# Decay masks of a Mamba-2 scan moved into the spare rows of its one-hot products, with a new order of work in two mixers of a four-block model

## The chip, the cores and the metric

One core of a Trainium2 chip runs the whole program in one launch. The metric is the time of the launch on the device in microseconds (us), less is better. TensorE is called PE below, VectorE DVE, ScalarE ACT, GpSimd POOL and SyncE SP.

## What is computed

256 tokens of width 1024 pass through two stacks of two layers. A layer of the first stack is a gated feed-forward, a mixer and another feed-forward; a layer of the second stack is one hybrid layer, which the change does not touch. The mixer adds three branches: a two-direction Mamba-2 scan (16 heads of 64, 2 groups, state 128, chunks of 128), latent attention of 8 heads, and a gated depthwise convolution. The reference of the scan, cut to what matters:

```python
x = x + 0.5 * swiglu(rms_norm(x, ffn1_norm[l]), ...)
u = rms_norm(x, mix_norm[l]) @ w_in[l]
z, xbc, dt_raw, q_lat, kv_lat, k_pe, c_h, c_b, c_c = jnp.split(u, pts, axis=-1)
...
# ssd_chunked, one direction; the second runs on flipped inputs
a_cs = jnp.cumsum(dtc * a, axis=2)
seg = a_cs[:, :, :, None] - a_cs[:, :, None, :]
decay = jnp.exp(jnp.where(lower, seg, -jnp.inf))
cb = jnp.einsum('bclgn,bcsgn->bclsg', cc, bc)
y_diag = jnp.einsum('bclsg,bclsgr,bcsgrp->bclgrp', cb, decay, xc * dtc[..., None])
decay_states = jnp.exp(a_cs[:, :, -1:] - a_cs)
states = jnp.einsum('bclgn,bclgr,bclgrp->bcgrpn', bc, decay_states, xd)
chunk_decay = jnp.exp(a_cs[:, :, -1])
...
y_off = jnp.einsum('bclgn,bcgrpn,bclgr->bclgrp', cc, prev, jnp.exp(a_cs))
```

## The kernel before

**Weights.** Every weight matrix comes in blocks of 512 KB. SP loads them into a ring of eight slots (RAW), ACT rounds a block (WH), DVE subtracts to get the rest (WL), both some five blocks ahead of PE, and PE multiplies three times (high by high, low by high, high by low). A block is 24 products of 256 columns or 12 of 512 and keeps PE busy for about 2.8 us. Its operands read XTH, XTL, WH and WL in the profile, FR in the mixer's output product. Other products are in plain fp32 or on rounded data.

**Order.** The class `Order` writes the order of all phases for all engines before the program is built. Chains of phases (`rows`, `decay`, `qk`, `mla_head`, `states`, `segment`, `finish` and so on in `mix`) are laid between the weight blocks. `WORK` gives each phase a duration per engine, `LEAD` each chain a lead, `RULE` the due times. An engine then works through its list strictly in order and waits on semaphores. In a mixer the phases that need a bank of PSUM take turns on banks 0 and 1, later 0, 1 and 3 (from `heads`), then 2 and 3 (after `mo_a` of the second half); weight blocks use banks 4 to 7.

**The attention** of a mixer runs head by head: `sc` (QTK,QTQ) makes scores, DVE finds their maximum (STATS), ACT takes exponentials (MP), `pt` transposes them (CONSTS,MP), ACT copies (MPT), `pv` multiplies by MV. `mo_a` divides (MO), and four flips transpose MO at the end.

**The scan.** `decay` makes dt (DT) and dt times a (DA). `cum` sums DA along the tokens by four products with triangles; ACT and DVE split the result into LBH. `ex` makes, by eight products of 16 columns, the sums that become the factors EX, and DVE makes the bias BI = ln dt - sum. `xs`, `btk` and `cbm` transpose the convolved input XC and form CB. `state` (XDD,BTK) and `fin` (STT,XC) carry the state across the chunks; DVE evicts `fin` to YT. `seg(n)`, n = 0 to 15, makes for two heads and both directions the decay matrix of 128 x 128: a product adds the mask (ROUNDED, 512 columns), two products spread the rows of LBH (256 columns each), then ACT takes four exponentials of 128 columns with the bias BI (ET), DVE adds the two directions and multiplies by CB. `apply(n)` multiplies by XS. The convolution branch has `cn_a` (CHC, RS, SPREAD), for which ACT takes a square root and DVE a reciprocal (RS).

In the profile L1190 is the helper of all products, L1187 that of all transposes, L1602 that of all activations, and L2068 the DVE split; the tiles tell them apart.

Of the kernel before, what the change touches and what calls it, by code (L numbers as in the profile page):

```python
# [58 lines left out]
def constants():  # L59
# [185 lines left out]
class Order:  # L245
# [307 lines left out]
    def mix(self, i, l):  # L553
# [315 lines left out]
class Kernel:  # L869
# [61 lines left out]
    def allocate(self):  # L931
# [216 lines left out]
class PE:  # L1148
# [229 lines left out]
    def cum(self, i):  # L1378
        k, w = self.k, self.w
        b, ps = self.tbank(("cum", i), "cum_dve", i)  # L1380
        w.wait_ge(*self.at("const6", 0))
# [1 line left out]
        for t in range(2):
            for d in range(2):
                m = self.mm(ps[:, 256 * t + 128 * d:256 * t + 128 * d + 128], k.DA[:, t, d, :], (k.LE, k.GE)[d],
                            t == 0 and d == 0, True)
        m.then_inc(*self.up("cum_pe", i))

    def ex(self, i):
        k = self.k  # L1390
        b, ps = self.tbank(("ex", i), "ex_dve", i)
        for t in range(2):
            for d in range(2):
                at = 64 * t + 32 * d
# [184 lines left out]
class Scalar:  # L1579
# [261 lines left out]
    def cum(self, i):  # L1841
# [1136 lines left out]
```

## Time and profile before

| | us |
|---|---|
| median of 3 runs (lowest, highest) | 1837.5 (1834.53, 1838.35) |
| the profiled execution | 1835.07 |
| its span | 1833.3 |
| PE busy | 1813.2 |
| DVE busy | 1263.2 |
| ACT busy | 1080.0 |
| POOL busy | 105.8 |

The granted clock of TensorE is 1.00 of full speed over the whole span. The mean DMA rate is 169 GB/s. The first mixer lies at about 192 to 404 us of the span, the second begins at about 769 us. In a row of the timeline the number after the start is the length of a group of instructions; matmuls overlap, so what a group costs is best read from its start to the start of the next group. A number in brackets is idle time of the engine before the group, and what ended it. fp32 products are two records each, so that "x8" of CONSTS,DA is four products.

### The profile page before, as it was taken

To read this page: it belongs to the slowest core of one execution; us is meant where nothing else is said; L and a number is where in the kernel's file an instruction comes from. 1 tells how busy PE (TensorE), PEld (TensorE's weight loads), DVE (VectorE), ACT (ScalarE), POOL (GpSimd) and SP (SyncE) were. 2 spreads that over 40 slices of the span, in tenths; PEclk is the share of its full clock that TensorE was granted. 3 is DMA by queue.
4 is the path that set the end of the run, shared out by engine and by line. 5 is a ranking of instruction groups with operands and counts; after the bars stand their busy time and mean duration, and the time that the engine had idled before them with its cause. 6 is when DMAs were issued, how large, how long until landed. Compare 5 with 4: busy or idle time off the path is not lost.

```text
span 1833.3 us, 28507 instructions
## 1 busy us (share of the span) xinstructions
PE 1813.2 (99%) x11518; PEld 1613.1 (88%) x11518; DVE 1263.2 (69%) x1932; ACT 1080.0 (59%) x1675; POOL 105.8 (6%) x83
## 2 busy tenths in 40 slices
PE   9999999999999999999999999999999999999999
PEld 9998998789998999899789998988778888887887
DVE  6765797876665665587876665687767567875755
ACT  6444667764444444575776444576776456668742
POOL 0000110010000000020000000002101000210100
PEclk9999999999999999999999999999999999999999
DMA  7565543245555555553335555554445555544463
GB/s 275 194 194 188 188 151 106 93 152 193 193 193 186 188 196 195 191 185 103 103 109 191 179 195 194 169 188 140 160 136 172 189 166 181 170 138 138 161 195 127
DMA packets 86596, 310.08 MB, mean 169 GB/s; under 512 B 9648, under 2 KB 10288, under 8 KB 86464
## 3 DMA queue, kind: packets, MB, share of 16 engines
q1 hardware_dynamic: 85680, 306.35, 50.5%
q8 instruction: 91, 1.49, 0.3%
q0 software_dynamic: 496, 1.65, 0.2%
q14 instruction: 41, 0.34, 0.1%
q10 hardware_dynamic: 288, 0.25, 0.0%
HBM read 307.16 MB, written 1.05 MB: 168 GB/s over the span
## 4 chain that ended last, share of the span: by engine, by line
PE 90%; ACT 5%; DVE 3%; issue 1%; DMA 0%; POOL 0%; SPq 0%; DVEq 0%; ACTq 0%
PE bank L1190 87%; PE bank L1187 3%; ACT PA L1602 2%; ACT WH L1602 1%; DVE WL L2068 1%; ACT L1602 1%; ACT ET L1602 1%; DVE PA L2721 0%; ACT MP L1602 0%; ACT FR L1602 0%; DMA X<-in_x_dram 0%; DVE PC L2746 0%; DVE STATS L2414 0%; ACT BZ L1602 0%; ACT ZS L1602 0%
## 5 line engine op out<-in xcount | busy, mean ns | idle before, releaser
L2068 DVE TENSOR_TENSOR WL<-RAW,WH 128x1024 fp32r<-128x1024 f32 x585 | 703.9, 1213 | 400.1 <-ACT WH L1602 398.5
L1602 ACT ACTIVATE WH<-RAW 128x1024 fp32r<-128x1024 f32 (+2 forms) x587 | 608.6, 1049 | 475.0 <-PE bank L1190 473.1
L1190 PE MATMUL bank<-WH,FR 128*128 128x512 f32 x1264 | 318.3, 390 | 1.4 <-ACT FR L1602 1.4
L1190 PEld LDWEIGHTS bank<-WH,FR 128*128 128x128 f32 x1264 | 233.8, 188 | 48.4 <-issue 1.8
L1190 PE MATMUL bank<-XTH,WH 128*128 128x256 f32 x1792 | 254.1, 279 | 0.6 <-ACT XTH L1602 0.6
L1190 PE MATMUL bank<-XTH,WL 128*128 128x256 f32 x1792 | 251.0, 277 | 0.0
L1190 PE MATMUL bank<-XTL,WH 128*128 128x256 f32 x1792 | 250.9, 277 | 0.0
L1190 PEld LDWEIGHTS bank<-XTH,WH 128*128 128x128 f32 x1792 | 226.9, 188 | 1.7 <-issue 0.8
L1190 PEld LDWEIGHTS bank<-XTL,WH 128*128 128x128 f32 x1792 | 225.8, 188 | 0.0
L1190 PEld LDWEIGHTS bank<-XTH,WL 128*128 128x128 f32 x1792 | 225.8, 188 | 0.0
L1190 PE MATMUL bank<-WL,FR 128*128 128x512 f32 x632 | 173.1, 388 | 0.0
L1190 PE MATMUL bank<-WH,XTHS 128*128 128x512 f32 x576 | 165.3, 398 | 2.5 <-ACT WH L1602 2.5
L1190 PE MATMUL bank<-WL,XTHS 128*128 128x512 f32 x576 | 160.3, 390 | 0.1
L1190 PE MATMUL bank<-WH,XTLS 128*128 128x512 f32 x576 | 160.2, 390 | 0.0
L1190 PEld LDWEIGHTS bank<-WL,FR 128*128 128x128 f32 x632 | 118.4, 188 | 24.6
L1190 PEld LDWEIGHTS bank<-WL,XTHS 128*128 128x128 f32 x576 | 108.0, 188 | 23.7 <-DVE WL L2068 1.0
L1190 PEld LDWEIGHTS bank<-WH,XTLS 128*128 128x128 f32 x576 | 108.1, 188 | 23.1
L1190 PEld LDWEIGHTS bank<-WH,XTHS 128*128 128x128 f32 x576 | 104.0, 188 | 24.6 <-ACT WH L1602 3.4
L2822 POOL TENSOR_TENSOR STATS<-STATS,HALFS 128x1 f32<-128x1 f32 (+2 forms) x36 | 68.8, 1921 | 683.5 <-DVE STATS L2763 191.0
L1602 ACT ACT_TABLE_LOAD x49 | 62.9, 1283 | 2.5 <-PEq L2969 1.7
L2253 DVE SCALAR_TENSOR_TENSOR XC<-XBG,COLP,XC 128x256 f32<-128x256 f32 x96 | 46.5, 484 | 8.6 <-ACT XC L1602 5.6
L1602 ACT ACTIVATE PA<-PA,STATS 128x128 f32<-128x128 f32 x64 | 34.2, 536 | 24.0 <-DVE STATS L2727 24.0
(328 smaller groups left out, 1827.3 us busy)
## 6 DMA issues: line engine op xcount, KB each, us to landing
RAW<-in_WALL_dram SPq DMA_DIRECT2D x569, 512.0 KB, 3.3
RAW<-in_WALL_dram SPq DMA_DIRECT2D x8, 448.0 KB, 3.3
RAW<-in_WALL_dram SPq DMA_DIRECT2D x8, 256.0 KB, 2.9
X<-in_x_dram SPq DMA_DIRECT2D x4, 256.0 KB, 5.4
out_dram<-X SPq DMA_DIRECT2D x4, 256.0 KB, 2.0
ROWP<-in_ROWP_dram POOLq DMA_DIRECT2D x1, 672.0 KB, 11.5
CONSTS<-in_CST_dram POOLq DMA_DIRECT2D x1, 664.0 KB, 7.8
ROUNDED<-in_CSTR_dram POOLq DMA_DIRECT2D x1, 208.0 KB, 12.7
```

Of the source, the lines that this page charges most:

```text
L1187: return self.e.transpose(out, in_, self.k.EYE[0:rows, 0:rows])
L1190: return self.e.matmul(out, lhs, rhs, start=start, stop=stop, skip_group_check=True)
L1602: return self.e.activation(out, in_, func, **k)
L2068: self.e.tensor_tensor(lo, raw, hi.bitcast(F32), ALU.subtract).then_inc(*self.up("lo", j))
L2253: e.scalar_tensor_tensor(o, src[:, tap:tap + 256], k.col("ssd_conv_w", l, 12 * tap + ch), o, ALU.mult, ALU.add).then_inc(*self.up("conv_dv ...
L2822: self.e.tensor_tensor(st, st, k.HM[:, 0:n], ALU.pow).then_inc(*self.up("rsqrt_pool", key))
```

## The change

`seg` no longer has a mask product and a bias. The one-hot stationary tiles are replaced by TOX and FROMX, 16 x 128 columns each, whose 64 spare rows hold "runs"; the other operands LBT and LBF hold the split sums in their used rows and the cut values in their spare rows. Four products of 256 columns give the whole exponent, and ACT takes one exponential of 512 columns. `cum` now adds ln dt inside the product (eight fp32 products instead of four) and is evicted in two halves by ACT and DVE. `ex` does both tiles in one product (four products of 32 columns instead of eight of 16), and its DVE step is gone. `decay` writes ln dt and dt times a into more places. POOL loads TOX, FROMX and the constant rows of LBF and LBT (2.4 MB in four DMAs) in each mixer, after the last two `sc`, in the phase `scan_load`; every `seg` waits for them. The leads of all chains of the mixer and its rule are new numbers; `heads` waits for `cum` instead of `ex`, and `ex` comes ahead of `cum`.

```diff
@@ def scan_constants
+    ends = [(1, 2)] + [(2 * j, 2 * j + 2) for j in range(1, 63)] + [(126, 127)]
+    runs = np.stack([(i >= a) & (i <= b) for a, b in ends]).astype(np.float32)
...
+        for p in (64 * x, 64 * x + 32):
+            s[x, p + i[:16], i[:16]] = 1
+        s[x, 64 * (1 - x):64 * (1 - x) + 64] = runs[:, None, :]
...
@@ WORK
-    "cum": "P90 A60 V70", "ex": "P170 A27 V20", ... "seg": "P56 A104 V90"
+    "cum": "P198 A105 V140", "ex": "P90 A27", ... "seg": "P50 A61 V90"
@@ LEAD["mix"], RULE
-        "qk": 1670, "mla_head": 180, "rope1": -470, "decay": 150, "states": 210, "segment": 70, "finish": 10, ...
+        "qk": -860, "mla_head": 230, "rope1": 1250, "decay": -10, "states": 220, "segment": -130, "finish": -110, ...
-RULE = {"ffn": (60, 240, 40), "mix": (400, 0, 60), "hyb": (500, 0, 20)}
+RULE = {"ffn": (60, 240, 40), "mix": (360, 0, 60), "hyb": (500, 0, 20)}
@@ Order.mix
+            yield [("ex", i)]
             yield [("cum", i)]
-            yield [("ex", i)]
...
-            yield "ex", i
+            yield "cum", i
...
-            yield [("mo_a", i, 1), ("tbanks", (2, 3))]
+            yield [("mo_a", i, 1), ("scan_load", i), ("tbanks", (2, 3))]
@@ PE.cum
+        w.wait_ge(*self.at("decay_act", (i, "ln")))
+                self.mm(o, k.DA[:, t, d, :], (k.LE, k.GE)[d], t == 0 and d == 0, False)
+                m = self.mm(o, k.LN[:, t, d, :], k.EYE, False, True)
@@ PE.ex
-                self.mm(ps[:, at:at + 16], (k.LE, k.GE)[d], k.DA[:, t, d, 0:16], t == 0 and d == 0, True)
-                m = self.mm(ps[:, at + 16:at + 32], (k.GT, k.LT)[d], k.DA[:, t, d, 0:16], False, True)
+                m = self.mm(out[:, :, d, a, :], tri, k.DA[:, :, d, 0:16], d == 0 and a == 0, True)
@@ PE.seg
-        w.wait_ge(*self.at("const5", 0))
-        self.mm(ps, k.EYER, k.CUT.unsqueeze(2).to_broadcast([128, 2, 2, 128]), True, False)
+        w.wait_ge(*self.at("scan_in", i))
         for x in range(2):
-            m = self.mm(ps[:, :, x, :], k.TO[:, h0 + x:h0 + x + 1].to_broadcast([128, 128]),
-                        k.LBH[:, 256 * t:256 * t + 256].rearrange("p (d s) -> p d s", d=2), False, x == 1)
+            self.mm(ps[:, :, x, :], k.TOX[:, h0 + x, :], k.LBT[:, 256 * t:256 * t + 256].rearrange("p (d s) -> p d s", d=2),
+                    x == 0, False)
+        for d in range(2):
+            m = self.mm(ps[:, d, :, :], k.LBF[:, 256 * t + 128 * d:256 * t + 128 * d + 128], k.FROMX[:, h0:h0 + 2, :], False, d == 1)
@@ Scalar.cum, Scalar.seg
-        self.act(k.LBH[:, :], ps[:, :], ACT.Copy).then_inc(*self.up("cum_act", i))
+        self.act(k.LBT[0:64, :], ps[0:64, :], ACT.Copy)
+        self.act(k.LBF[64:128, :], ps[64:128, :], ACT.Copy).then_inc(*self.up("cum_act", i))
...
-                m = self.act(k.ET[:, n % 4, at:at + 128], k.PS[k.bank["seg", i, n]][:, at:at + 128], ACT.Exp,
-                             bias=k.BI[:, t, d, h:h + 1])
+        self.act(k.ET[:, n % 4, :], k.PS[k.bank["seg", i, n]][:, :], ACT.Exp).then_inc(*self.up("et_act", (i, n)))
@@ Vector.ex (gone)
-        e.tensor_tensor(k.BI, k.BI, ps, ALU.subtract).then_inc(*self.up("ex_dve", i))
@@ Pool.scan_load
+        for h in (6, 7):
+            w.wait_ge(*self.at("sc_pe", (i, h)))
+        w.wait_ge(*self.at("cum_pe", i))
+        w.wait_ge(*self.at("kpe_pool", (i, 1)))
+        e.dma_start(k.TOX[:, :, :], src[:, 0:2048].rearrange("p (h s) -> p h s", h=16)).then_inc(*k.sig.landed("scan_in"))
+        e.dma_start(k.FROMX[:, :, :], src[:, 2048:4096].rearrange("p (h s) -> p h s", h=16)).then_inc(*k.sig.landed("scan_in"))
+        e.dma_start(k.LBF[0:64, :], src[0:64, 4096:4608]).then_inc(*k.sig.landed("scan_in"))
+        e.dma_start(k.LBT[64:128, :], src[64:128, 4096:4608]).then_inc(*k.sig.landed("scan_in", i))
```

What the new numbers do to the order of work is seen in the instruction lists. The first place is PE at the end of the attention of a mixer. QTK,QTQ is `sc`, CONSTS,MP `pt`, MV,MPT `pv`, CONSTS,XC `xs` (and `btk`), XC by XC `cbm`, and WH or WL by XTH a weight block. Before:

```order
L1187 MATMUL bank<-CONSTS,XC 128x128 x8
L1190 MATMUL bank<-WH,XTH 128x512 x4
L1190 MATMUL bank<-WH,XTL 128x512 x4
L1190 MATMUL bank<-WL,XTH 128x512 x4
L1187 MATMUL bank<-CONSTS,XC 128x128 x8
L1190 MATMUL bank<-WH,XTH 128x512 x4
L1190 MATMUL bank<-WH,XTL 128x512 x4
L1190 MATMUL bank<-WL,XTH 128x512 x4
L1187 MATMUL bank<-CONSTS,XC 128x128 x4
L1190 MATMUL bank<-XC 128x128 x4
```

Now, from the last `sc` on (third row):

```order
L1212 MATMUL bank<-WL,XTH 128x512 x2
L1209 MATMUL bank<-CONSTS,MP 128x128 x4
L1212 MATMUL bank<-QTK,QTQ 128x256 x2
L1209 MATMUL bank<-CONSTS,XC 128x128 x8
L1212 MATMUL bank<-MV,MPT 128x64 x8
L1209 MATMUL bank<-CONSTS,MP 128x128 x8
L1209 MATMUL bank<-CONSTS,XC 128x128 x8
L1212 MATMUL bank<-MV,MPT 128x64 x4
L1209 MATMUL bank<-CONSTS,XC 128x128 x4
L1212 MATMUL bank<-XC 128x128 x4
L1212 MATMUL bank<-MV,MPT 128x64 x4
```

A weight block stood between any two groups of transposes. Now no weight block stands between the last `sc` and the last `pv`, and the last `pt` and `pv` stand among the transposes of XC.

The second place is ACT beside it, again before and now. XC<-XC is the silu of the convolution, for which ACT loads a table; BTK, CB and ZS are copies and the silu of banks that PE filled. Before:

```order
L1602 ACTIVATE WH<-RAW 128x1024
L1602 ACTIVATE CW<-PR,COLP 128x256
L1602 ACT_TABLE_LOAD
L1602 ACTIVATE XC<-XC 128x1024
L1602 ACTIVATE MOQ<-MO 128x512 x2
L1602 ACTIVATE WH<-RAW 128x1024
L1602 ACTIVATE XS<-bank 128x512 x2
L1602 ACTIVATE XC<-XC 128x1024
L1602 ACTIVATE CW<-PR,COLP 128x256
L1602 ACTIVATE WH<-RAW 128x1024
L1602 ACTIVATE XS<-bank 128x512 x2
L1602 ACTIVATE WH<-RAW 128x1024
```

Now:

```order
L1626 ACTIVATE MPT<-bank 128x512
L1626 ACTIVATE MP,STATS<-bank,STATS 128x256 x2
L1626 ACTIVATE XS<-bank 128x512 x2
L1626 ACT_TABLE_LOAD
L1626 ACTIVATE XC<-XC 128x1024
L1626 ACTIVATE MPT<-bank 128x512 x2
L1626 ACTIVATE XS<-bank 128x512 x2
L1626 ACTIVATE CW<-PR,COLP 128x256
L1626 ACTIVATE BTK<-bank 128x512
L1626 ACTIVATE CB<-bank 128x512
L1626 ACTIVATE CW<-PR,COLP 128x256
L1626 ACTIVATE ZS<-bank,SUMS 128x512 x2
```

The silu and its table load stood ahead of the first XS and with no MP or MPT behind them; now they stand between the exponentials of the last head (MP) and the two last MPT. The silu ZS, which frees banks 6 and 7 for the next weight blocks, comes at the end of this list.

The third place is DVE a little later, where the states are made. YT<-bank evicts `fin`, RS<-bank evicts the bank of CHC, FR and WL belong to weight blocks. Before:

```order
L2465 TENSOR_TENSOR SPT<-DT,EX 128x16
L2469 TENSOR_TENSOR XDD<-XS,SPT 128x1024
L2081 SCALAR_TENSOR_TENSOR FR<-bank,COLP,FR 128x256 x4
L2263 SCALAR_TENSOR_TENSOR CW<-PR,COLP,CW 128x256 x2
L2477 TENSOR_TENSOR YT<-bank,EX 128x512 x2
L2210 TENSOR_TENSOR CW<-bank,CW 128x512 x2
L2500 TENSOR_TENSOR XK<-XS,ROWP 128x1024
L2068 TENSOR_TENSOR WL<-RAW,WH 128x1024
L2500 TENSOR_TENSOR XK<-XS,ROWP 128x1024
L2508 TENSOR_TENSOR YT<-XK,YT 128x1024
L2068 TENSOR_TENSOR WL<-RAW,WH 128x1024
L2477 TENSOR_TENSOR YT<-bank,EX 128x512 x2
```

Now:

```order
L2229 TENSOR_TENSOR CW<-bank,CW 128x512 x2
L2087 TENSOR_TENSOR WL<-RAW,WH 128x1024
L2482 TENSOR_TENSOR SPT<-DT,EX 128x16
L2486 TENSOR_TENSOR XDD<-XS,SPT 128x1024
L2465 TENSOR_TENSOR MO<-MO,STATS 128x512 x2
L2517 TENSOR_TENSOR XK<-XS,ROWP 128x1024
L2087 TENSOR_TENSOR WL<-RAW,WH 128x1024
L2353 SCALAR_TENSOR_TENSOR RS<-bank,RBC 128x256
L2356 TENSOR_SCALAR RS<-RS 128x256
L2358 RECIPROCAL RS<-RS 128x256
L2360 TENSOR_TENSOR RS<-RS,RBC 128x256
L2494 TENSOR_TENSOR YT<-bank,EX 128x512 x2
```

The eviction YT stood ahead of the work on RS; now it stands behind it and its reciprocal, and RS itself behind two MO, one XK and one WL.

## Rows read from the trace of the kernel before

**Rows 1.** The page: busy time, share of the span and instructions of each engine.
```profile
PE 1813.2 (99%) x11518; PEld 1613.1 (88%) x11518; DVE 1263.2 (69%) x1932; ACT 1080.0 (59%) x1675; POOL 105.8 (6%) x83
```

**Rows 2.** Windows view, 290 to 340 us: length, busy of each engine, clock, DMA share, GB/s.
```profile
290.00:340.00 50.00, 48.31 (x269) 37.44 (x267) 42.92 (x65) 37.55 (x60) 3.33 (x2) 1.00 0.32 106
```

**Rows 3.** Timeline of PE around cum and ex: start, length, engine, line, operation, tiles, count.
```profile
228.54 1.05 PE L1190 MATMUL bank<-CONSTS,DA 128*128 128x128 f32 x8
229.35 0.71 PE L1190 MATMUL bank<-WH,FR 128*128 128x512 f32 x2
...
247.36 1.85 PE L1190 MATMUL bank<-DA,CONSTS 128*128 128x16 f32 x16
249.06 1.19 PE L1190 MATMUL bank<-XTH,WH 128*128 128x256 f32 x8
250.09 1.10 PE L1190 MATMUL bank<-XTL,WH 128*128 128x256 f32 x8
```

**Rows 4.** Timeline of PE in the run of segs, same columns.
```profile
352.99 0.55 PE L1190 MATMUL bank<-XS,ET 128*128 128x64 f32 x4
353.35 0.48 PE L1190 MATMUL bank<-ROUNDED 128*128 128x512 f32 x1
353.67 0.39 PE L1190 MATMUL bank<-LBH,ROUNDED 128*128 128x256 f32 x2
353.89 0.55 PE L1190 MATMUL bank<-XS,ET 128*128 128x64 f32 x4
...
357.52 0.39 PE L1190 MATMUL bank<-ROUNDED 128*128 128x512 f32 x1
...
365.68 2.02 PE L1190 MATMUL bank<-WH,FR 128*128 128x512 f32 x8
```

**Rows 5.** Timeline of ACT in the same run.
```profile
355.91 11.11 ACT L1602 ACTIVATE ET<-bank,SPT 128x128 f32<-128x128 f32 x40
```

**Rows 6.** Waits of PE, 190 to 405 us: releaser, total us, times, longest.
```profile
PE bank L1190 <- ACT FR L1602: 0.6, 1, 0.6
PE bank L1187 <- ACT QTK L1602: 0.3, 1, 0.3
PE bank L1187 <- ACT MP L1602: 0.3, 1, 0.3
```

**Rows 7.** Timeline of PE where the STT product waits.
```profile
319.79 0.66 PE L1187 MATMUL bank<-CONSTS,MO 128*128 128x128 f32 x4 [0.20 <-ACT STT L1602]
321.43 1.99 PE L1190 MATMUL bank<-STT,XC 128*128 128x512 f32 x4 [0.98 <-DVE FR L2081]
```

**Rows 8.** Chain of waits around 289 us: start, us, engine and tile, count.
```profile
289.49 1.21 ACT MP L1602 x4
```

**Rows 9.** Timeline of ACT, 300 to 323 us.
```profile
300.95 0.50 ACT L1602 ACTIVATE CW<-PR,COLP 128x256 f32<-128x256 f32 x1
301.47 1.28 ACT L1602 ACT_TABLE_LOAD   x1
302.76 1.06 ACT L1602 ACTIVATE XC<-XC 128x1024 f32<-128x1024 f32 x1
...
321.61 1.26 ACT L1602 ACTIVATE ZS<-bank,SUMS 128x512 f32<-128x512 f32 x2
```

**Rows 10.** Timeline of DVE, 287 to 358 us.
```profile
287.00 0.69 DVE L2414 TENSOR_REDUCE STATS<-bank 128x2 f32<-128x512 f32 x1 [1.03 <-PE bank L1190]
...
314.79 1.22 DVE L2469 TENSOR_TENSOR XDD<-XS,SPT 128x1024 f32<-128x1024 f32 x1
...
335.44 1.75 DVE L2335 RECIPROCAL RS<-RS 128x256 f32<-128x256 f32 x1 [0.48 <-ACT RS L1602]
...
357.07 0.43 DVE L2488 TENSOR_TENSOR ET<-ET 128x256 f32<-128x256 f32 x1 [1.82 <-ACT ET L1602]
```

**Rows 11.** The page: the POOL-issued DMA queue, and one of its issues with us to landing.
```profile
q0 software_dynamic: 496, 1.65, 0.2%
...
ROUNDED<-in_CSTR_dram POOLq DMA_DIRECT2D x1, 208.0 KB, 12.7
```

More of the change, by code:

```diff
@@ L83, in constants, with scan_constants @@
     return np.ascontiguousarray(c, np.float32), g, r
+def scan_constants():
+    ends = [(1, 2)] + [(2 * j, 2 * j + 2) for j in range(1, 63)] + [(126, 127)]
+    i = np.arange(128)
+    runs = np.stack([(i >= a) & (i <= b) for a, b in ends]).astype(np.float32)
+    s = np.zeros((2, 128, 16, 128), np.float32)
+    for x in range(2):
+        for p in (64 * x, 64 * x + 32):
+            s[x, p + i[:16], i[:16]] = 1
+        s[x, 64 * (1 - x):64 * (1 - x) + 64] = runs[:, None, :]
+    cut = np.zeros((128, 2, 2, 128), np.float32)
+    for k, (a, b) in enumerate(ends):
+        cut[64 + k, :, 0] = np.where(i < a, -1e30, 0.0)
+        cut[64 + k, :, 1] = np.where(i > b, -1e30, 0.0)
+        cut[k, :, 0] = np.where(i > b, -1e30, 0.0)
+        cut[k, :, 1] = np.where(i < a, -1e30, 0.0)
+    return np.ascontiguousarray(np.concatenate([s[0].reshape(128, 2048), s[1].reshape(128, 2048), cut.reshape(128, 512)], 1))
 class Signals:
@@ L213 @@
     "mix": {
-        "qk": 1670, "mla_head": 180, "rope1": -470, "decay": 150, "states": 210, "segment": 70, "finish": 10, "flips":
-        640, "conv": -80, "conv2": -30, "evicted": -10, "sums": -1390, "kpe": -1920, "skip": -230, "heads": 160,
-        "lat": 150, "cn": 70, "rows": 100,
+        "qk": -860, "mla_head": 230, "rope1": 1250, "decay": -10, "states": 220, "segment": -130, "finish": -110,
+        "flips": 80, "conv": 160, "conv2": 300, "evicted": 170, "sums": -320, "kpe": 80, "skip": 270, "heads": 190,
+        "lat": 140, "cn": 220, "rows": 530,
     },
@@ L1007, in allocate @@
         assert x <= p2
-        self.LBH, x = mk("LBH", [128, 512], p1, F32R)
+        self.LBT, x = mk("LBT", [128, 512], p1, F32R)
+        self.TOX, _ = mk("TOX", [128, 16, 128], 0, F32R)
+        self.FROMX, _ = mk("FROMX", [128, 16, 128], 16384, F32R)
         self.ET, _ = mk("ET", [128, 4, 512], 32768)
@@ L1380, in cum, with ex @@
         b, ps = self.tbank(("cum", i), "cum_dve", i)
+        w.wait_ge(*self.at("decay_act", (i, "ln")))
+        for t in range(2):
+            for d in range(2):
+                o = ps[:, 256 * t + 128 * d:256 * t + 128 * d + 128]
+                self.mm(o, k.DA[:, t, d, :], (k.LE, k.GE)[d], t == 0 and d == 0, False)
+                m = self.mm(o, k.LN[:, t, d, :], k.EYE, False, True)
+        m.then_inc(*self.up("cum_pe", i))
+    def ex(self, i):
+        k, w = self.k, self.w
+        b, ps = self.tbank(("ex", i), "ex_act", i)
         w.wait_ge(*self.at("const6", 0))
         w.wait_ge(*self.at("decay_dve", (i, 3)))
[L1383 to L1394, printed above, removed]
-                self.mm(ps[:, at:at + 16], (k.LE, k.GE)[d], k.DA[:, t, d, 0:16], t == 0 and d == 0, True)
-                m = self.mm(ps[:, at + 16:at + 32], (k.GT, k.LT)[d], k.DA[:, t, d, 0:16], False, True)
+        out = ps[:, 0:128].rearrange("p (t d a h) -> p t d a h", t=2, d=2, a=2)
+        for d in range(2):
+            for a, tri in enumerate(((k.LE, k.GT), (k.GE, k.LT))[d]):
+                m = self.mm(out[:, :, d, a, :], tri, k.DA[:, :, d, 0:16], d == 0 and a == 0, True)
         m.then_inc(*self.up("ex_pe", i))
@@ L1765, in decay @@
             w.wait_ge(*self.at("decay_dve", (i, "ln")))
-            self.act(k.BI, k.BI, ACT.Ln).then_inc(*self.up("decay_act", (i, "ln")))
+            self.act(k.LN[:, :, :, 64:80], k.LN[:, :, :, 64:80], ACT.Ln)
+            self.act(k.LN[:, :, :, 96:112], k.LN[:, :, :, 96:112], ACT.Ln).then_inc(*self.up("decay_act", (i, "ln")))
     def lat_sq(self, i, t):
@@ L2311, in decay @@
             w.wait_ge(*self.at("pads_pool", i))
-            e.tensor_scalar(k.BI, k.DT[:, :, :].rearrange("p t (d h) -> p t d h", d=2), 1e-18, None, ALU.max).then_inc(
-                *self.up("decay_dve", (i, "ln")))
+            for at in (64, 96):
+                m = e.tensor_scalar(k.LN[:, :, :, at:at + 16], k.DT[:, :, :].rearrange("p t (d h) -> p t d h", d=2), 1e-18, None, ALU.max)
+            m.then_inc(*self.up("decay_dve", (i, "ln")))
             for d in range(2):
                 a = k.SPT[:, 5, 16 * d:16 * d + 16].unsqueeze(1).to_broadcast([128, 2, 16])
-                for at in (0, 32):
-                    m = e.scalar_tensor_tensor(k.DA[:, :, d, at:at + 16], k.DT[:, :, 16 * d:16 * d + 16], -1.0, a, ALU.mult, ALU.mult)
+                e.tensor_tensor(k.DA[:, :, d, 64:80], k.DT[:, :, 16 * d:16 * d + 16], a, ALU.mult).then_inc(*self.up("decay_dve"))
+            w.wait_ge(*self.now("decay_dve"))
+            for d in range(2):
+                for at, sgn in ((96, 1.0), (0, -1.0), (32, -1.0)):
+                    m = e.tensor_scalar(k.DA[:, :, d, at:at + 16], k.DA[:, :, d, 64:80], sgn, None, ALU.mult)
             m.then_inc(*self.up("decay_dve", (i, 3)))
@@ L2830, in mix_pads @@
         e.memset(k.PR[:, :, 257:258], 0.0)
+        e.memset(k.LN[:, :, :, :], 0.0)
         e.memset(k.DA[:, :, :, :], 0.0).then_inc(*self.up("pads_pool", i))
```

27 lines of the change are left out of this document (11 added, 16 removed), and 4 rows, old and new, of the table WORK.

## The prediction

> **What bounds the kernel now.** I read the page first: PE is busy 99% of the span, DVE 69% [rows 1]. So the time is the sum of what PE executes plus some 20 us in which it stands idle. Nothing can help but fewer or cheaper products, or fewer waits of PE. The loads are far from the limit: between 290 and 340 us the DMA engines are busy for 0.32 of the time [rows 2]. The same row shows where the change acts: PE stands for 1.7 of the 50 us, and DVE is busy for 42.9, ACT for 37.6. In the mixers both helpers are near full, so there their lists, which run strictly in order, decide when PE may go on. I then read the timeline of PE for the prices of products, the run of segs for its pace, the waits for what is lost today, and the timelines of ACT and DVE for the length of each thing in their lists.
>
> **The products themselves (per mixer).** A removed product costs what its start-to-start time shows. `ex`: eight products of 16 columns take 247.36 to 249.06, 1.70 us or 0.21 each [rows 3]. Four products of 128 columns (`cum`) take 228.54 to 229.35, 0.81 or 0.20 each. So a small fp32 product costs the same at 16 and at 128 columns; the four of 32 that replace `ex` cost 0.85, which saves 0.85. `cum` has four more, which costs 0.81. A change from fp32 to rounded products costs another tenth: the pass of eight at 249.06 takes 1.03, where eight of a quarter of the LBH pair's kind take 0.9 (353.67 to 353.89 is two in 0.22) [rows 3, 4]. The new order has three such changes fewer, -0.3. A `seg` has 512 + 256 + 256 columns before and 4 x 256 now, the same 1024: 0, as the cover is PE's rate per column; if a product has a cost of its own, one more per seg is at most 16 times some hundredths, 0 to +0.5. Sum -0.3 (range -0.4 to +0.3).
>
> **The run of segs.** From 357.52 to 365.68 PE does eight segs and seven applies in 8.16 us. Without waits an apply takes 0.36 (352.99 to 353.35) and a seg behind it 0.54 (353.35 to 353.89) [rows 4]: 6.8 us. So 1.4 us are lost to the four exponentials of a seg, of which ACT does 40 in 11.11 us, 1.1 us per seg [rows 5]. Now a seg needs one activation of 512 columns, 0.6 by the nearest row (ZS, two in 1.26) [rows 9]. The pace goes to PE's own 0.90 or to DVE's two steps, which follow one another at 0.4 to 0.5 each [rows 10], 0.9: the 1.4 go. The run now has eleven segs with no weight block ahead of the first apply but two more segs, 1.0 us of work; exponential and two steps take 1.5 with their hand-overs 1.7: +0.7. Sum -0.7 (range -1.4 to +0.3).
>
> **Waits of today that the order takes away.** Behind the flips of MO, STT,XC starts 1.64 after the second pair, of which its own work is 0.44, and 0.2 more is lost ahead of the pair [rows 7]. That is 1.4, and both groups have moved: -1.4 (range -1.4 to 0, since something must stand there now). ACT's late FR costs 0.6 and meets a lighter ACT: -0.6 (0 at worst). The attention loses 0.3 and 0.3 to QTK and MP [rows 6]; the new leads put two to three blocks between scores and exponentials in its middle: -0.4 (range -0.6 to +0.6). Sum -2.4.
>
> **Waits that the order brings.** I followed the three lists shown above, from the end of the last `sc`.
> First, banks and ACT. The third group of XC transposes needs the bank of the next-to-last `pt`, so it needs the first MPT of the pair behind the table load. ACT's list to there: DVE's maximum 0.8 [rows 10], MP 1.2 [rows 8], two XS 1.1, table load 1.28, silu 1.0, MPT 0.6 at ZS's price [rows 9]: 6.0 us. PE has meanwhile two groups of four transposes twice (1.6), two `pv` (0.8) and 0.4 of a group: 2.9. It loses about 2.9 us.
> Second, the next weight block needs the banks that ZS frees. From the MPT on, ACT has MPT, two XS, CW, BTK, CB, CW and the first ZS, eight pieces of 0.4 to 0.6, 3.8 us; PE has five groups of 0.42, 2.1. It loses 1.7.
> Third, the second STT,XC needs the bank of CHC, evicted by the RS at the eighth row of DVE's new list. From the last `pv` on, DVE does MO 0.7, XDD 1.3, CW 0.9, the sums over MOQ 1.7, CW 1.2, WL 1.2, XDD 1.3, two MO 1.2, XK 1.2, WL 1.2 and RS 0.4 (these run at about 0.6 per 512 columns, as XDD's 1.22 for 1024 [rows 10]): 12.3. PE has the loss just named, two blocks of 2.8, XDD 1.7, CHC 0.7 and half an STT 0.7: 10.4. It loses 1.9.
> Fourth, the flips of MO need the bank that YT frees, now behind RS, ACT's square root, the reciprocal of 1.75 [rows 10] and one step: 3.5 with YT, against 0.7 of PE's own. It loses 2.8.
> Together 9.3. Each leg is an upper bound, since an engine that catches up in one wait is earlier at the next and groups of PE pass at a tenth less in a row; below, the same stretch loses 2 us today. I take three quarters, 6.8 (range 2 to 9.3), nearer to the reckoning, because every piece in it is in program order and has a measured length.
> [...] In the trace CW starts at 300.95 for 0.50, the load at 301.47, the silu at 302.76 [rows 9]: a switch costs 1.3 us in all. [...]
>
> **Moved or added, at nothing.** One BI step of DVE falls, six short ones in `decay` and one longer eviction come, about 1 us in a stretch in which PE has only weight blocks ahead of it; uncovered it would cost 1. The order of POOL gets four DMA issues and a memset; its queue is empty most of the time (106 us busy of 1833). The transfers share the engines with the weights, whose ring is full: no cost while they end in time (below).
>
> **Sum.** Per mixer -0.3 - 0.7 - 2.4 + 6.8 = +3.4, twice +6.8. The profiled execution was 1835.07 (span 1833.3 and 1.8 around it), so 1841.9 by its measure. It is 2.4 under the median of its runs, 1837.5, so 1844.3 by the median's. I forecast **1844**, slower by 6.5.
>
> **Rivals.**
> *The helpers arrive early (no measurable change).* The legs overlap more than I take them to: ACT and DVE shed the ET work (ACT 0.5 us per seg, 8 per mixer) and enter the cluster ahead. At 3.4 instead of 6.8 the mixer is even: 1837.5. For it: today's reckoning of the same kind finds DVE at 43 of 50, not 50. Against it: the segs come after the cluster, so what they shed helps only later.
> *The order fits and the scan is lighter (faster).* The same four waits come to 1.0 per mixer and the gains stand in full: -2.4 per mixer, 1832.7. The place is the pair of MPT behind the silu and the YT behind the reciprocal; the point from which it decides is a total under 2.5 us per mixer, beneath which the time falls by more than can be told. For it: the removed 1.4 in the run and the removed 1.4 before STT are seen in rows, the added waits in none.
> *The tables come late (much slower).* All segs wait for 2.4 MB. At the start POOL's queue moved 1.65 MB, its last part landing 12.7 us after its issue [rows 11], beside full-rate weight loads; by that rate 2.4 MB take about 20 us. Between the last `sc` and the first seg PE has some 31 us (five to six blocks at 2.8, the small groups above, the new waits on top). It decides from a rate below 76 GB/s; at 60 it costs 9 us per mixer, 1862. [...]
> *The mask product was not the cost.* If DVE's two steps pace the segs, the run gains nothing: +2.8, 1847, inside the range.
>
> **Chances.** Forecast's case 0.45, with the last rival 0.03 beside it; helpers early 0.27; faster 0.20; tables late 0.05. A measurement of this kernel tells 0.2% (3.7 us) from nothing. Slower by more takes 0.48, the first, the last and the late tables less 0.05 of the forecast's case near its lower edge; within 0.2% takes 0.30 and faster 0.22, which hold that 0.05 beside their own. The range holds 8 in 10: 1831 (the faster case with its bounds) to 1851 (legs in full, 9.3, gives 1849, and unknown products 2); the forecast's own range is 1840 to 1851.
>
> **What would show it.** In the new profile: (1) PE idle behind ACT MPT or XS near the last `pv`, then behind ACT ZS, then behind DVE RS and YT: about 7 us per mixer; (2) ET at 0.6 each and the segs at 0.9 us per pair with an apply; (3) no wait for TOX or FROMX, their DMAs landed some 10 us before the first seg; (4) `ex` 0.85 and `cum` 1.6; (5) the feed-forward and hybrid stretches unchanged. If (1) is under 2.5 us per mixer, the forecast is wrong and the order is better than my reading of it; if PE waits at the first seg on a DMA, the late tables are right.

## The result and the profile after

| | before | changed |
|---|---|---|
| median of the runs (lowest, highest), us | 1837.41 (1834.53, 1838.35) | 1858.5 (1857.65, 1860.94) |
| ratio to before, 95% interval | | 1.0125 [1.0113, 1.0137] |
| the profiled execution's span, us | 1833.3 | 1856.9 |
| PE busy in it, us | 1813.2 | 1822.5 |
| mean granted clock | 1.00 | 0.994 |
| first mixer, from its first x flip to the next stage's last, us | 213.1 | 225.2 |
| second mixer, likewise, us | 213.3 | 225.1 |

The change makes the kernel slower by 21 us by these medians, three times what was forecast, and the time lies above the stated range. The two profiled executions differ by 23.6 us, and all of that falls in the two mixers, 12 us in each; the other stages take what they took. The two mixers are measured between the same transposes of X before (194.02 to 407.09) and after (193.48 to 418.63). The page of the changed kernel, busy times and the queue of POOL's transfers, answers to [rows 1, 11]:

```profile
PE 1822.5 (98%) x11550; PEld 1622.0 (87%) x11550; DVE 1266.6 (68%) x1942; ACT 1074.0 (58%) x1587; POOL 106.0 (6%) x93
...
q0 software_dynamic: 1392, 6.37, 1.0%
```

The waits of PE in the first mixer (releaser, total us, times, longest) answer to [rows 6]:

```profile
PE bank L1212 <- DVE RS L2356: 2.1, 1, 2.1
PE bank L1209 <- ACT MPT L1626: 2.1, 1, 2.1
PE bank L1209 <- ACT MP L1626: 1.8, 1, 1.8
PE bank L1209 <- DVE YT L2494: 1.2, 1, 1.2
PE bank L1209 <- ACT QTQ L1626: 1.0, 1, 1.0
PE bank L1212 <- ACT ZS L1626: 0.9, 1, 0.9
```

These six hold 9.2 us in one mixer. QTK and MP had been 0.3 each before. Now MPT, MP and ZS (the end of the attention) and RS and YT (the states) lead. All but MP are names that the prediction had followed.

The timeline of PE shows where they stand. The columns are start, length, engine, line, operation, tiles and count. From the last scores on:

```profile
308.72 1.03 PE L1212 MATMUL bank<-QTK,QTQ 96*128 96x256 f32 x4
309.59 1.04 PE L1209 MATMUL bank<-CONSTS,XC 128*128 128x128 f32 x8
...
314.19 1.14 PE L1209 MATMUL bank<-CONSTS,MP 128*128 128x128 f32 x8 [1.83 <-ACT MP L1626]
315.17 0.72 PE L1209 MATMUL bank<-CONSTS,XC 128*128 128x128 f32 x4
318.02 1.11 PE L1209 MATMUL bank<-CONSTS,XC 128*128 128x128 f32 x4 [2.13 <-ACT MPT L1626]
318.93 1.81 PE L1212 MATMUL bank<-MV,MPT 128*128 128x64 f32 x8
...
322.78 1.00 PE L1212 MATMUL bank<-MV,MPT 128*128 128x64 f32 x8
324.70 1.45 PE L1212 MATMUL bank<-WH,XTH 128*128 128x512 f32 x4 [0.91 <-ACT ZS L1626]
```

and at the states:

```profile
333.05 1.13 PE L1212 MATMUL bank<-STT,XC 128*128 128x512 f32 x2
336.30 2.07 PE L1212 MATMUL bank<-STT,XC 128*128 128x512 f32 x2 [2.13 <-DVE RS L2356]
339.60 1.97 PE L1209 MATMUL bank<-CONSTS,MO 128*128 128x128 f32 x8 [1.23 <-DVE YT L2494]
341.22 1.95 PE L1212 MATMUL bank<-WH,XTH 128*128 128x512 f32 x4
```

The last scores start at 308.72. The pair of `pt` waits 1.83 for ACT, the third group of XC transposes 2.13, the first weight block 0.91. Then the second STT,XC waits 2.13 for RS and the flips of MO 1.23 for YT. Besides, the same work has become dearer in places in which PE does not wait: MV,MPT x8 is 1.81 long at 318.93 and 1.00 at 322.78, and CONSTS,MO x8 takes 1.62 (339.60 to 341.22) where eight transposes of XC at 309.59 take 0.87. The windows of 2 us there (length, busy of PE, PEld, DVE, ACT, POOL, then the granted clock, the DMA share and GB/s):

```profile
312.00:314.00 2.00, 0.36 (x4) 0.22 (x2) 0.87 (x3) 1.06 (x4) 0.25 (x1) 1.00 0.92 344
314.00:316.00 2.00, 1.70 (x12) 1.26 (x12) 0.00 (x0) 1.98 (x5) 0.00 (x0) 0.90 1.06 418
316.00:318.00 2.00, 0.00 (x0) 0.00 (x0) 0.00 (x0) 1.99 (x4) 0.00 (x0) 0.50 1.11 330
318.00:320.00 2.00, 1.98 (x10) 1.98 (x11) 0.00 (x0) 1.77 (x4) 0.00 (x0) 0.50 0.19 35
320.00:322.00 2.00, 2.00 (x11) 2.00 (x11) 1.08 (x3) 0.54 (x2) 0.00 (x0) 0.50 0.00 0
322.00:324.00 2.00, 1.79 (x15) 1.65 (x13) 0.10 (x1) 1.24 (x4) 0.00 (x0) 0.89 0.00 0
...
336.00:342.00 6.00, 4.47 (x12) 2.81 (x13) 5.48 (x7) 2.60 (x6) 0.00 (x0) 0.51 0.00 0
```

PE had worked without a pause until 312. It is then idle for most of 312 to 314, and for all of 316 to 318. The granted clock is 0.90 on average from 314 to 316 and 0.50 from 316 on: it falls to half at about 315.6, shortly before the second idle time begins (315.9). It returns within 322 to 324, and PE has been busy since 318.02 by then. The last row is the second such stretch, behind the wait on RS.

The list of DVE behind the two places:

```profile
310.88 1.22 DVE L2087 TENSOR_TENSOR WL<-RAW,WH 128x1024 fp32r<-128x1024 f32 x1
312.02 0.68 DVE L2437 TENSOR_REDUCE STATS<-bank 128x2 f32<-128x512 f32 x1
...
335.50 0.42 DVE L2353 SCALAR_TENSOR_TENSOR RS<-bank,RBC 128x256 f32<-128x256 f32 x1
...
336.73 1.75 DVE L2358 RECIPROCAL RS<-RS 128x256 f32<-128x256 f32 x1 [0.48 <-ACT RS L1626]
...
338.86 1.28 DVE L2494 TENSOR_TENSOR YT<-bank,EX 128x512 f32<-128x512 f32 x2
```

and the list of ACT:

```profile
312.94 0.56 ACT L1626 ACTIVATE MP<-bank,STATS 128x256 f32<-128x256 f32 x1 [3.42 <-DVE STATS L2440]
...
315.13 1.28 ACT L1626 ACT_TABLE_LOAD   x1
316.43 1.06 ACT L1626 ACTIVATE XC<-XC 128x1024 f32<-128x1024 f32 x1
317.39 1.07 ACT L1626 ACTIVATE MPT<-bank 128x512 f32<-128x512 f32 x2
```

PE ends the last scores at 309.59, but DVE takes their maximum only at 312.02, behind two splits and a CW. ACT's exponentials come at 312.94, and MPT, behind the table load and the silu, at 317.39. RS is evicted at 335.50 and YT at 338.86, after the reciprocal of 1.75.

The scan itself does what it was meant to do. In the run of segs, where [rows 4] had a pace of 1.0 to 1.3 us, a seg with its apply now takes 0.92:

```profile
358.98 0.48 PE L1212 MATMUL bank<-LBT,TOX 128*128 128x256 f32 x2
...
359.90 0.48 PE L1212 MATMUL bank<-LBT,TOX 128*128 128x256 f32 x2
```

### The profile page after: what moved, and what is told of

Its sections match the earlier page's. It is cut to its first block, busy times and chain, and to the rows that moved or that the text cites. A ratio compares the mean times of both kernels' runs of the same rounds, so it can differ in the third digit from the quotient of the medians.

```text
span 1856.9 us, 28505 instructions
## 1 busy us (share of the span) xinstructions
PE 1822.5 (98%) x11550; PEld 1622.0 (87%) x11550; DVE 1266.6 (68%) x1942; ACT 1074.0 (58%) x1587; POOL 106.0 (6%) x93
## 4 chain that ended last, share of the span: by engine, by line
PE 91%; DVE 4%; ACT 4%; issue 1%; DMA 0%; POOL 0%; SPq 0%; DVEq 0%; ACTq 0%
PE bank L1212 87%; PE bank L1209 3%; ACT PA L1626 2%; DVE WL L2087 1%; ACT L1626 1%; ACT WH L1626 1%; DVE PA L2738 0%; ACT MP L1626 0%; DMA X<-in_x_dram 0%; DVE CW L2282 0%; DVE RS L2358 0%; DVE PC L2763 0%; DVE XC L2272 0%; DVE STATS L2437 0%; ACT BZ L1626 0%
## 5 line engine op out<-in xcount | busy, mean ns | idle before, releaser
L1212 PEld LDWEIGHTS bank<-XTH,WL 128*128 128x128 f32 x1792 | 226.0, 188 | 0.0
L1212 PEld LDWEIGHTS bank<-XTL,WH 128*128 128x128 f32 x1792 | 225.9, 188 | 0.0
```

Of the source, the lines that this page charges most:

```text
L1212: return self.e.matmul(out, lhs, rhs, start=start, stop=stop, skip_group_check=True)
```

## The experiments

Each run is compared with the kernel before on the same chip (medians of it 1834.96 to 1835.36). "Mixer" is the length of the first and second mixer in the profiled execution, between the same x flips as above.

| run | us | ratio to before [95%] | mixers, us | clock |
|---|---|---|---|---|
| e1 changed scan, old leads | 1860.5 | 1.0136 [1.0121, 1.0152] | 225.8, 225.9 | 0.994 |
| e2 old scan, new leads | 1850.6 | 1.0083 [1.0066, 1.0100] | 221.0, 220.9 | 0.996 |
| e4 fillers, too long | 1857.0 | 1.0119 [1.0104, 1.0134] | 224.0, 224.2 | 1.000 |
| e6 changed scan, old order | 1832.9 | 0.9984 [0.9975, 0.9993] | 211.5, 211.6 | 1.000 |
| e7 fillers, sized | 1853.0 | 1.0092 [1.0077, 1.0107] | 222.0, 222.0 | 1.000 |
| e8 cn_a moved | 1860.1 | 1.0127 [1.0110, 1.0144] | 226.0, 225.9 | 0.993 |
| e9 a block moved | 1858.9 | 1.0120 [1.0102, 1.0137] | 225.2, 223.0 | 0.995 |
| e10 both moved | 1858.7 | 1.0124 [1.0106, 1.0143] | 224.3, 224.1 | 0.995 |
| e11 three blocks back | 1851.9 | 1.0094 [1.0079, 1.0109] | 220.8, 221.4 | 0.996 |
| e12 three blocks early, old order | 1840.0 | 1.0027 [1.0017, 1.0037] | 216.4, 213.7 | 0.998 |
| e13 five blocks back | 1846.0 | 1.0054 [1.0039, 1.0070] | 217.9, 217.6 | 1.000 |
| e14 old order, one block later | 1840.5 | 1.0028 [1.0019, 1.0038] | 216.6, 215.4 | 0.997 |

### Leads against code

**e1** took the changed kernel and put the mixer's old leads and rule back:

```diff
-        "qk": -860, "mla_head": 230, "rope1": 1250, "decay": -10, "states": 220, "segment": -130, ...
+        "qk": 1670, "mla_head": 180, "rope1": -470, "decay": 150, "states": 210, "segment": 70, ...
-RULE = {..., "mix": (360, 0, 60), ...}
+RULE = {..., "mix": (400, 0, 60), ...}
```

> The changed scan (masks in the spare rows, one exponential per bank, cum and ex in their new form, the tables loaded in each mixer) with the leads and the rule of the mixer as they were before. Theory A (the new order makes the 12 us that each mixer lost; the scan code itself costs nothing or gains 1 to 2 us per mixer): 1832 to 1839 us. Rival B (the scan code or its 2.4 MB of tables per mixer is what costs): 1850 us or more.

It took 1860.5, which by that expectation speaks for the code. **e2** was the other half, the kernel before with the new leads and rule:

> The kernel before with only the leads and the rule of the mixer replaced by the new ones; masks, biases, cum, ex stay as before and no table is loaded. Theory A (the order): slower than before by 10 to 25 us, 1848 to 1862, with idle of PE behind ACT MPT, DVE RS and DVE YT and stretches at a granted clock of 0.5. Rival B (the scan code): 1835 to 1840.

It took 1850.6, which speaks for the order. The two together say that the pair was badly cut: a lead is only one input of `Order`. The durations in `WORK` (cum, ex and seg are new) and the phase that the heads wait for also moved, so e1 did not have the old order, nor e2 the new one. The waits tell the same: e1 stands behind CW, XBG, QTQ and ZS, none of which leads in either kernel.

Neither run is explained by what the next sections find at the last scores. In the trace both have five weight blocks among the scores and seven behind them, close to the five and six of the kernel before, and yet their mixers take 225.8 and 221.0. The two longest waits of e1 lie elsewhere, ahead of the scores (XBG, 1.9 at 262.5) and in the run of segs (CW, 1.9 at 361.2), and behind each its granted clock is at 0.50 for some us (from 264 to 266 and from 364 to 368). So an order can lose as much at other places.

**e6** therefore pinned the order itself. It gives `Order` all its old inputs, lets it write the phases of before, and only then exchanges cum and ex (the evicted sums lie where ex reads DA) and adds the loads behind the last scores:

```diff
     order = Order(STAGES)
+    other = {"cum": "ex", "ex": "cum"}
+    order.phases = [(other[p[0]], *p[1:]) if p[0] in other else p for p in order.phases]
```

> The changed scan code in the order of work of the kernel before, phase by phase (only cum and ex have changed places, since the evicted sums now overwrite what ex reads, and the four table loads follow the last scores). The first two runs left open whether the scan code costs anything, since the old leads with the new durations gave 1860.5 and the new leads with the old scan code 1850.6: neither kept an order. Theory A (order alone): 1829 to 1834 us, faster than before by 1 to 4 us per mixer's run of segs and unloaded ACT. Rival B (the scan code costs by itself, by its tables or the longer cum): 1845 us or more. In between (1835 to 1840): the exponentials were hidden by other work.

It took 1832.9, 0.9984 of before with an interval below one: the changed scan in the old order beats both kernels, the kernel before by 2.4 us. So the order alone costs the rest, from 211.5 to 225.1 in each mixer. The run of segs shows the gain. Eight segs and seven applies take 6.98 us here (358.98 to 365.96), where before they took 8.16 [rows 4]:

```profile
358.98 0.40 PE L1212 MATMUL bank<-LBT,TOX 128*128 128x256 f32 x2
...
365.96 1.31 PE L1212 MATMUL bank<-WH,FR 128*128 128x512 f32 x5
```

The windows of e6 over the states and over the segs, same columns as above:

```profile
290.00:340.00 50.00, 48.31 (x277) 38.21 (x276) 42.10 (x65) 37.69 (x61) 5.53 (x6) 1.00 0.46 151
340.00:375.00 35.00, 35.00 (x215) 30.30 (x214) 27.55 (x54) 22.08 (x37) 1.11 (x2) 1.00 0.36 118
```

From 290 to 340 PE is busy 48.31 of 50, as before [rows 2], although POOL loads the tables there. From 340 to 375 PE has no idle at all. The 2.4 MB cost nothing that can be seen: in the changed kernel the loads are issued at 310 to 312, each lands 6 to 8 us later, and the first seg starts at 356:

```profile
TOX<-in_CSTX_dram POOLq DMA_DIRECT2D x1, 1024.0 KB, 6.1
FROMX<-in_CSTX_dram POOLq DMA_DIRECT2D x1, 1024.0 KB, 7.6
...
LBT<-in_CSTX_dram POOLq DMA_DIRECT2D x1, 128.0 KB, 8.2
```

This settles the rival of the late tables. In e6 the four loads are issued from 294.7 to 296.4 and the last lands at 304.7; DVE is busy for some 7.5 of these 10 us, and the first seg, at 335, does not wait.

### What the clock costs

**e4** filled PE's waits with repeats of products whose result stays the same:

```diff
-        for x in range(4):
-            m = self.tr(ps[:, 128 * x:128 * x + 128], k.XC[:, c + x, 128 * t:128 * t + 128])
+        for again in range({(0, 0): 3, (0, 4): 3, (1, 0): 6}.get((t, c), 1)):
+            for x in range(4):
+                m = self.tr(ps[:, 128 * x:128 * x + 128], k.XC[:, c + x, 128 * t:128 * t + 128])
...
+        for again in range({(0, 0): 5, (0, 1): 3}.get((t, g), 0)):
+            self.mm(ps[:, :], k.XC[:, 10 + g, 128 * t:128 * t + 128], k.STT[:, g, :], True, True)
```

> The changed kernel with products repeated where PE would stand (the same transposes of XC two more times for the first two groups, five more times for the third; the same STT product five more times ahead of the first and three more ahead of the second), some 5.5 us more of PE work per mixer laid into its waits. Same results. Theory C (half of what was not foreseen is TensorE's clock, which falls to half after the waits and makes the products behind them dearer by 4 to 5 us per mixer): the granted clock stays 1.00 and the kernel is faster than the changed one by 5 to 10 us, 1848 to 1854. Rival D (the clock follows the waits without costing more than they do): at 1858 to 1861, no faster, or slower by what the repeats overshoot the waits.

The clock stayed at 1.00, but the time fell by 1.5 only. An STT product costs 0.85, twice what I had sized it at, so the eight repeats ran 2.8 us past the release of YT. The result lay between both expectations and decided nothing. **e7** is the same with `{(0, 0): 2, (0, 1): 3}` in the second place:

> The fillers of the last run with the STT product repeated two and three times (it had been five and three, which overshot: 0.85 us each, the run ended 2.8 us behind the release of the bank). Theory C (the clock's fall costs 3 to 4 us per mixer beyond the waits): the granted clock stays at 1.00 and the kernel takes 1850 to 1853 us. Rival D (the fall costs nothing beyond the waits): 1857 to 1860.

It took 1853.0. Two windows of it, where the changed kernel had a clock of 0.50:

```profile
314.00:318.00 4.00, 3.91 (x36) 3.63 (x35) 0.00 (x0) 3.97 (x7) 0.00 (x0) 1.00 1.08 408
318.00:322.00 4.00, 3.98 (x36) 3.68 (x34) 1.08 (x3) 3.43 (x8) 0.00 (x0) 1.00 0.16 27
```

With some 8 us more of PE work in each mixer the kernel is 5.5 us faster. So the fall of the clock costs at least 2.8 us per mixer, 3.1 by the length of the mixers, beyond the waits that came before it. The waits themselves stay: the fillers only sit in them. With the clock at 1.00 throughout, the new order still takes 222.0 per mixer against 211.5 in e6, so most of the loss is not the clock's.

### Single places

**e8** moved the phase cn_a (first pair of lines), **e9** the last weight block of the first half of z (second pair), **e10** both, each in both mixers:

```diff
     order = Order(STAGES)
+    for i in (1, 4):
+        order.phases.remove(("cn_a", i))
+        order.phases.insert(order.phases.index(("flip", "mo", i, 10, 2)) + 1, ("cn_a", i))
+        it = last_z(i)
+        order.phases.remove(it)
+        order.phases.insert(order.phases.index(("pv", i, 5)) + 1, it)
```

> The changed kernel with one phase moved in each mixer: cn_a (CHC, and on ACT and DVE the work on RS with its reciprocal) goes behind the flips of MO. Theory A (single places of the new order cost what their waits and the clock behind them show): the waits on DVE RS (2.1 to 2.9) and on YT (1.2 to 2.2) and the half-speed stretch behind them go, 3 to 5 us per mixer, 1848 to 1853 us. Rival E (DVE as a whole is late there, so that the waits only change their name): 1856 or more.

> The changed kernel with one weight block moved in each mixer, from ahead of the last scores to behind the two pv that follow them. Theory A: the wait on MP (1.8) is filled with the block's 2.8 us of useful work, the pair of pt starts with its exponentials done, and the clock falls later or not at all: 2 to 4 us per mixer, 1850 to 1855. Rival E (the helpers are late as a whole): 1856 or more.

> Both moves together. Theory A: the gains add up, 5 to 9 us per mixer, 1841 to 1849 us. Rival E: they don't, 1853 or more.

They took 1860.1, 1858.9 and 1858.7, the last two with a spread of 7 to 8 us from run to run. None is told from the changed kernel. In e8 the waits on RS and on YT of the first mixer (2.1 and 1.2) became these:

```profile
PE bank L1212 <- DVE FR L2100: 2.4, 1, 2.4
PE bank L1209 <- DVE YT L2494: 2.0, 1, 2.0
```

That is 4.4 us where there had been 3.3. The flips of MO start 3.8 us earlier (335.84 instead of 339.60), but CHC, now behind them, waits for DVE in turn, and the clock falls there as it did before (0.50 from 340 to 344): RS was only the last of what DVE had to do before PE could go on. In e9 the wait on MP went from 1.8 to 0.3, MPT rose from 2.1 to 3.4, and the first mixer kept its 225.2 us (the second took 223.0). So a wait that is named in the profile was no handle by itself. My reading was that it stands for a long list of ACT and DVE in order, with too little else for PE to do beside it.

### The work beside the list

Counting the weight blocks in the phases gives that a shape. Between the first and the last scores PE has 5 blocks before and 10 now; between the last scores and the flips of MO 6 before and 2 now. A block is 2.8 us, so 11 us of work left the stretch in which the helpers are slowest. **e11** keeps the new order and puts three blocks back behind the last scores:

```diff
-  sc7, block 99, block 100, splits, block 101, ..., pt4, sc6, xs, xs, pv4, pv5, silu, pt7, pt6, xs, xs, ...
+  sc7, pt4, sc6, block 99, xs, xs, pv4, pv5, block 100, pt7, pt6, silu, block 101, xs, xs, ...
```

> The last runs left the mechanism: single waits only changed their name. Theory F: from the last scores to the flips of MO, ACT and DVE have a chain of some 28 to 30 us (27.6 from start to start before, 30.9 in the changed kernel) that is about as long in every order; before, PE has six weight blocks (17 us) to do beside it, in the new order two, since it has done ten instead of five among the scores. This run leaves the new leads and puts three blocks, with their splits, from ahead of the last scores to behind them, so that five stand beside the chain. F: 6 to 9 us of the idle and half-speed time go in each mixer that has them, so 1841 to 1849 us. Rival G (it is the number of transposes and small products in a row, or the changed scan, that sets the loss): 1855 or more.

**e12** is the mirror in the old order: of its six blocks three go ahead of the last scores.

```diff
-  pt4, sc6, pv4, pv5, pt7, pt6, block 96, splits, ..., block 97, split, ..., block 98, ...
+  pt4, block 96, splits, block 97, split, block 98, sc6, pv4, pv5, pt7, pt6, ...
```

> The mirror of it, in the order of before with the changed scan (the kernel that took 1832.9): three of the six blocks that stand behind the last scores are put ahead of them, with their splits; nothing else moves. F: 5 to 9 us per mixer are lost, 1842 to 1851 us, with idle of PE behind MP, MPT or XC, and stretches of the granted clock under 1. Rival G: 1832 to 1836 us.

Both moved the way of theory F, by about half of what it expected, and both lie outside its ranges. e11 took 1851.9, 6.6 less than the changed kernel, and e12 1840.0, 7.1 more than e6 (the clock is at 0.50 from 308 to 314 in it). The waits of e11 in the first mixer:

```profile
PE bank L1212 <- DVE RS L2356: 2.1, 1, 2.1
PE bank L1209 <- DVE YT L2494: 1.2, 1, 1.2
...
PE bank L1209 <- ACT MP L1626: 0.9, 1, 0.9
```

MP fell from 1.8 to 0.9 and MPT is gone; the half-speed stretch there went with them (the granted clock is 1.00 until 330); RS and YT stand as they were, with a half-speed stretch behind them (332 to 340), since all three blocks lie ahead of the last `pv`. In e12 waits appear that neither e6 nor the kernel before has, at the place that lost its blocks:

```profile
PE bank L1209 <- ACT XC L1626: 1.7, 1, 1.7
...
PE bank L1212 <- ACT MPT L1626: 0.7, 1, 0.7
```

**e13** adds to e11 two blocks ahead of the flips of MO, one between CHC and the first STT,XC, one behind it.

> The kernel with three blocks back behind the last scores (1851.9), and in each mixer the next two weight blocks also put ahead of the flips of MO: one between CHC and the first STT,XC, one between these and the flips. Seven blocks now stand between the last scores and the flips. Theory F: the waits on DVE RS (2.1) and YT (1.2) and the half-speed stretch behind them (2.8) are covered; what comes behind the flips has two blocks fewer and may lose 1 to 3 us at XDD, SPREAD and the first seg. 2 to 5 us per mixer: 1842 to 1848. Rival E (the waits change their name again): 1850 or more.

1846.0, inside what was expected: the waits on RS and YT are down to 1.3 on FR and 0.3 on YT, the clock is 1.00 throughout, and the mixer is 217.9. Seven of the 12 us are back. The remainder, 6.4 against e6, is spread over waits of 0.2 to 1.3 at many places (QTQ, MP, XS, ZS, FR and the first segs lead); I did not take it apart.

**e14** asked whether more blocks beside the list are always better. In e6 the block ahead of the last scores goes behind the two `pv` after them, so that seven stand there:

> The changed scan in the old order (1832.9) with the weight block ahead of the last scores moved behind the two pv after them. By theory F one more block beside the chain covers the wait on MP (0.5 us per mixer): 1831 to 1832.5 us. If the block is missed where it was: 1833 to 1835.

They are not: 1840.5, 7.5 slower than e6. The timeline of PE among the scores, where the block is now missing:

```profile
288.55 0.66 PE L1209 MATMUL bank<-CONSTS,MP 128*128 128x128 f32 x4 [0.91 <-ACT MP L1626]
...
291.56 3.67 PE L1212 MATMUL bank<-MV,MPT 128*128 128x64 f32 x16 [1.39 <-ACT MPT L1626]
294.99 2.05 PE L1212 MATMUL bank<-XTH,WH 128*128 128x256 f32 x8
```

and its window, columns as above:

```profile
292.00:296.00 4.00, 4.00 (x21) 4.00 (x21) 2.25 (x5) 1.20 (x4) 0.67 (x2) 0.50 0.97 352
```

PE waits there 0.9 for MP and 1.4 for MPT, and then MV,MPT x16 takes 3.4 us from start to start and the first pass of a block 1.9, both about twice their price (1.7 and 1.0), at a clock of 0.50. So the count of blocks behind the last scores is at most half of the rule; the heads need theirs as well, and e1 and e2 show that even both counts together do not vouch for an order. The part of theory F by which the helpers' list is as long in every order is also wrong: from the last scores to the flips it took 27.6 us before, 30.9 in the changed kernel, 33.9 and 35.1 in e11 and e13, 24.2 in e12.

## Why the prediction was wrong

**The direction was right, the size was not**: +3.4 us per mixer was forecast, +12.1 measured. Losses are counted here from start to start against the same group undisturbed.

- *The products, -0.3.* About right. The segs cost the same, ex 0.8 and cum 1.7 (put at 1.6). The sum of the groups' own times, an estimate from undisturbed rows, falls by 0.28 per mixer.
- *The run of segs, -0.7.* Right: 0.92 per pair, and waits of 0.22 and 0.18 before the third seg and the first apply.
- *Waits that go away, -2.4.* The waits at STT, at FR, at MP and at CW went, -4.1 with the two hidden ones in the run. But QTQ grew by 0.7, RS,SPREAD has 0.7 that had not been there, and the start of the segs costs 0.7 more. With the run, the two parts had been put at -3.1 and came to -2.0: 1.1 of the error.
- *Waits that the order brings, +6.8.* This step failed. Followed the four legs had given 9.3; I took three quarters, arguing that the engines catch up from one leg to the next. PE lost about 9.6 us at the five places, 2.8 more than was forecast. But the full reckoning came near that sum by luck; leg by leg it was off: 4.3 (MP and MPT) where it had 2.9, 1.1 (ZS) where it had 1.7, 2.5 (RS) for 1.9, 1.7 (YT) for 2.8. The last three make 5.3 of 6.4, so there the discount was not far off. The step that failed is the first leg. Its list had DVE at hand for the maximum of the last scores; DVE came 2.4 us late, behind splits and a CW, so that the list lasted 8.4 us and not 6.0. PE had 4.1 us of work meanwhile and not 2.9, since two `pv` cost 1.8 and not 0.8, and part of the wait fell one group earlier, at MP. The switch of tables was no part of the miss: load and silu stand 1.30 apart here (315.13 to 316.43), as against 1.29 in [rows 9].
- *A term that was not there: the clock.* The working held PE's granted clock for given and had no price for products at half speed. In the rows of the first mixer the products at 0.50 cost 4.7 us more than their own time. By e7 some 3.1 us of these, at least, are time that a steady clock would give back; for the rest, up to 1.6, PE would have come to its releases earlier and waited longer.
- 1.1 + 2.8 + 4.7 make 8.6 of the 8.7 missed. Put by cause and not by row, the clock is about 3.1 of it and the waits about 4.4, the larger piece.
- Two slips in the working changed little: 6.0 less 2.9 is 3.1 for the first leg, and a total of 2.5 us in waits would have made the kernel faster by 1.8 us, which is less than the 3.7 that it says can be told.

**The rivals.** "The helpers arrive early" and "the order fits" assumed less than the reckoning; both fell. The gains on which the second rested were real but are worth 1.6 us per mixer, as e6 shows. "The tables come late" did not happen: there were 46 us between issue and first use (310 to 356), where the prediction had 31, and the last load had landed 8 us after its issue. "The mask product was not the cost" fell with the pace of 0.92. None of the cases, nor the upper end of 1851, held a price for PE at half speed. So even the legs in full gave 1849 and the range was too narrow on the side on which the reckoning leant.

**The sum as it stands after the runs**, per mixer: scan code in an unchanged order -1.6; order +13.6, of which 3.1 are the clock's; together about +12. That the order is the cause is shown by e6. Of the 13.6, e13 gives back 7.3 by moving five blocks; where the other 6.4 arise, beyond the waits named there, stays open.

## What to carry to other kernels

When a planner is given new durations and new leads at once, judge the code by pinning the old list of phases and changing only the code: here that turned 21 us slower into 2.4 us faster. Where PE is the bound and the helpers work in order, count the large products that stand beside each long helper list, before and now, as a first sign and not as a rule (five and seven blocks were no protection in e1 and e2). A wait that the profile names is only the last link, and moving a single phase, a block or both gave nothing that could be told. Where a hand-followed list says that PE will stand for whole microseconds, price also the products behind the waits at half the clock as a bound (0.50 was granted here), and ask for each helper what it is still busy with when its first piece falls due. The first leg was missed there.

## What the runs showed of the hardware

- The granted clock fell to 0.50 at about 315.6, after PE had been idle for 1.8 us and busy for 1.4, and again at about 336, while PE stood for 2.1 us after 9 us of nearly unbroken work. It came back at about 322.4 and 343, PE being busy since 318.02 and 339.60. MV,MPT x8 took 1.60 us from start to start at 0.50 (318.93), against about 0.84 at 1.00. In the kernel before it stood at 1.00 throughout both mixers.
- Some 8 us of useless products per mixer made the kernel 5.5 us faster (e7); the granted clock is 1.00 throughout there.
- The small fp32 products cost about the same at 16, 32 and 128 columns: four of 32 columns took 0.81 us (237.55 to 238.36 in the changed kernel), 0.20 each, where eight of 16 took 1.70, 0.21 each, and four of 128 took 0.81, 0.20 each [rows 3].
- Two loads of 1 MB, issued by POOL 0.6 us apart, landed after 6.1 and 7.6 us in the changed kernel, where all DMA together moved 418 GB/s from 314 to 316, and after 6.1 and 7.5 us in e6, where DVE was busy for 7.5 us from 294.7 to 304.7.
